# The first norm of a two-block layer stack: order of the identity, the norm weights' copy and the first square

## What is computed

```
def _rms_norm(x, g):
    xf = x.astype(jnp.float32)
    y = xf * lax.rsqrt(jnp.mean(xf * xf, axis=-1, keepdims=True) + EPS)
    return (y * g.astype(jnp.float32)).astype(x.dtype)

h = _rms_norm(x, g_pre_mix[l])
proj = h @ w_in[l]
qa, ka, va, c_q, c_kv, k_r, gate_logits = _split_cols(proj, ...)
...
x = x + _rms_norm(merged @ w_out[l], g_post_mix[l])
h2 = _rms_norm(x, g_pre_mlp[l])
m = jnp.square(jax.nn.relu(h2 @ w_up[l])) @ w_down[l]
x = x + _rms_norm(m, g_post_mlp[l])
...
return second_block(x, ...)
```

## Time and profile before

| | |
|---|---|
| Runs, median of 3 | 997.12 us (996.72 to 998.54) |
| The profiled execution | 995.95 us |
| its span in the profile | 994.2 us |
| PE busy | 978.6 us, 98% |
| DVE busy | 701.8 us, 71% |
| ACT busy | 480.0 us, 48% |
| POOL busy | 79.2 us, 8% |
| mean granted TensorE clock | 0.998 of full speed |

### The profile page before, as it was taken

The page is one execution under the profiler, slowest core; times in us unless marked ns, Lnnn a source line. Parts: engine busy times, 40 slices in busy tenths (PEclk is TensorE's granted clock), DMA queues, the critical chain, the costliest instruction groups (busy, mean ns, idle before and its releaser), DMA issues.

```text
span 994.2 us, 13319 instructions
## 1 busy us (share of the span) xinstructions
PE 978.6 (98%) x5444; PEld 851.5 (86%) x5444; DVE 701.8 (71%) x733; ACT 480.0 (48%) x558; POOL 79.2 (8%) x74
## 2 busy tenths in 40 slices
PE   8999999999999999999999999999989999999997
PEld 7888888888888888999988888888889888888886
DVE  5765657777766676567677876767789977767674
ACT  4667456554533455441235443434369745434342
POOL 0400000000000001008510000000013100000000
PEclk9999999999999999999999999999999999999999
DMA  7664424655555553652224755555245637555631
GB/s 268 228 253 161 162 87 149 212 212 186 195 202 208 183 212 142 239 171 85 85 85 162 263 187 196 184 193 193 85 148 178 248 141 266 184 196 181 201 121 42
DMA packets 27292, 176.35 MB, mean 177 GB/s; under 512 B 3416, under 2 KB 3680, under 8 KB 7648
## 3 DMA queue, kind: packets, MB, share of 16 engines
q1 hardware_dynamic: 27072, 175.44, 50.1%
q10 hardware_dynamic: 160, 0.07, 0.0%
HBM read 174.45 MB, written 1.05 MB: 177 GB/s over the span
## 4 chain that ended last, share of the span: by engine, by line
PE 87%; DVE 7%; ACT 2%; issue 2%; DMA 2%; POOL 0%; ACTq 0%; POOLq 0%; DVEq 0%; SPq 0%
PE ps L1682 20%; PE ps L1655 16%; PE ps L1657 16%; PE ps L1656 16%; PE ps L1685 10%; PE ps L2065 3%; DVE wL L995 2%; PE ps L1701 2%; DMA raw<-w_stream 1%; PE ps L1839 1%; ACT FF L558 1%; DVE FF L1587 1%; PE ps L1735 1%; PE ps L1849 1%; DVE RR L1007 1%
## 5 line engine op out<-in xcount | busy, mean ns | idle before, releaser
L995 DVE TENSOR_TENSOR wL<-raw,wH 128x2048 fp32r<-128x2048 f32 (+2 forms) x158 | 352.8, 2242 | 92.2 <-ACT wH L553 92.1
L553 ACT ACTIVATE wH<-raw 128x2048 fp32r<-128x2048 f32 (+2 forms) x158 | 292.7, 1859 | 121.2 <-PE ps L1685 54.3
L1682 PE MATMUL ps<-aHL,wH 128*128 128x512 f32 x864 | 215.8, 392 | 0.0
L1682 PEld LDWEIGHTS ps<-aHL,wH 128*128 128x128 f32 x864 | 157.2, 189 | 29.4
L1655 PE MATMUL ps<-wL,RR 128*128 128x512 f32 (+1 forms) x384 | 150.2, 391 | 0.4 <-DVE RR L1007 0.4
L1656 PE MATMUL ps<-wH,RR 128*128 128x512 f32 (+1 forms) x384 | 149.2, 389 | 0.0
L1657 PE MATMUL ps<-wH,RR 128*128 128x512 f32 (+1 forms) x384 | 148.9, 388 | 0.0
L1685 PEld LDWEIGHTS ps<-aHL,wL 128*128 128x128 f32 x864 | 117.9, 190 | 8.4
L1685 PE MATMUL ps<-aHL,wL 128*128 128x256 f32 x864 | 120.5, 282 | 0.0
L1655 PE MATMUL ps<-wL,aHL 128*128 128x512 f32 (+2 forms) x296 | 119.1, 402 | 0.2 <-ACT xn L567 0.2
L1657 PE MATMUL ps<-wH,aHL 128*128 128x512 f32 (+2 forms) x296 | 114.0, 385 | 0.0
(11 more groups left out here) (237 smaller groups left out, 1138.2 us busy)
## 6 DMA issues: line engine op xcount, KB each, us to landing
raw<-w_stream SPq DMA_DIRECT2D x152, 1024.0 KB, 4.9
raw<-w_stream SPq DMA_DIRECT2D x6, 512.0 KB, 4.6
FF<-rows_in SPq DMA_DIRECT2D x5, 512.0 KB, 6.9
raw<-w_stream SPq DMA_DIRECT2D x4, 576.0 KB, 5.4
bc<-rows_in SPq DMA_DIRECT2D x4, 512.0 KB, 7.5
xr<-x_in SPq DMA_DIRECT2D x2, 512.0 KB, 4.0
xn<-rows_in SPq DMA_DIRECT2D x1, 1024.0 KB, 4.8
out<-xn SPq DMA_DIRECT2D x4, 256.0 KB, 2.2
```

The costliest lines, as they stand in the source:

```text
L553: e.activation(weight_slot(i)[0][:, 0:wd], raw[:, slot, 0:wd], ACT.Copy).then_inc(hi, 1)
L995: e.tensor_tensor(l[:, 0:wd], raw[:, slot, 0:wd], h[:, 0:wd].bitcast(F32), ALU.subtract).then_inc(lo, 1)
L1682: e.matmul(ps[:, b, :], h[:, cs[k]], aHL[:, k].rearrange("p i t -> p (i t)"), start=k == 0, stop=False)
```

## The change

Three places are written in another order, and the number of products of zeros goes from 11 to 12. ACT issues the identity first and the norm weights second. ACT takes the first square (tile 0) ahead of the copy of the turned norm weights, while the squares of tile 1 stay behind it. PE makes eight products of zeros, waits for x's first tile, makes two more, then the gain product, then two more; before, it made six, the gain product, two, waited for x's first tile, and made three. All waits and all other instructions of the kernel are kept.

```
--- before.py
+++ after.py
@@ -567,8 +567,8 @@
                 e.activation(dst, ps[:, bank, 0:width], ACT.Copy).then_inc(copied, 1)
 
 
+            e.dma_start(ident[:, :], const_d[:, 0:128]).then_inc(id_in, 16)
             e.dma_start(gain_rows, rows_d[R_PRE_MIX:R_PRE_MIX + 1024].rearrange("(k p) -> k p", k=8)).then_inc(gain_in, 16)
-            e.dma_start(ident[:, :], const_d[:, 0:128]).then_inc(id_in, 16)
             e.wait_ge(dve_own, 2)
             e.activation(consts[:, 2:3], consts[:, 1:2], ACT.Square).then_inc(act_own, 1)
 
@@ -584,10 +584,10 @@
                 e.wait_ge(gained, GAINED["mix", t, g])
                 e.activation(aH[:, 4 * g:4 * g + 4, TOK[t]], plain_rows[:, t, 4 * g:4 * g + 4], ACT.Copy).then_inc(flip_hi, 1)
 
+            e.wait_ge(x_in[0], 16)
+            square(("mix", 0, 0), first_out[:, 0], xr[:, 0, 0:512])
             e.wait_ge(gain_out, 1)
             e.activation(gain_cols, ps[:, 7, 0:8], ACT.Copy).then_inc(gain_act, 1)
-            e.wait_ge(x_in[0], 16)
-            square(("mix", 0, 0), first_out[:, 0], xr[:, 0, 0:512])
             e.wait_ge(x_in[1], 16)
             for c in range(2):
                 square(("mix", 1, c), first_out[:, 2 + c], xr[:, 1, 512 * c:512 * c + 512])
@@ -1716,13 +1716,13 @@
                     e.matmul(ps[:, 0, 0:128], warm, warm, start=True, stop=True)
 
             e.wait_ge(warm_in, 1)
-            warm_up(6)
+            warm_up(8)
+            e.wait_ge(x_in[0], 16)
+            warm_up(2)
             e.wait_ge(gain_in, 16)
             e.wait_ge(id_in, 16)
             e.matmul(ps[:, 7, 0:8], gain_rows, ident[0:8, 0:8], start=True, stop=True).then_inc(gain_out, 1)
             warm_up(2)
-            e.wait_ge(x_in[0], 16)
-            warm_up(3)
 
 
             ck = a_at("w_in", 1536, 384, 8)
```

## The result

The changed kernel took 993.27 us (median of 5 runs, 992.86 to 994.21) against 997.12 for the kernel before (5 runs, 996.23 to 998.80) on the same chip: a ratio of 0.9959, with a 95% interval of 0.9945 to 0.9974. Measured again beside other kernels it was 993.48 (9 runs) against 996.39 (28 runs), ratio 0.9973 (0.9963 to 0.9983). So it is 2.9 to 3.9 us faster. The lower end is the better figure: of the kernel before there are 70 runs beside the experiments, with a median of 996.50, and the five here, with 997.12, lie above it. The forecast was 994.9 and 2.2 us, with a range of 993.5 to 996.5: the direction was right, the saving too small, and the time is 0.2 us outside the range.

What follows compares the result with a forecast made beforehand. PE was taken as the bound, its front strung on the identity's transfer. Shift 2.1 us plus 0.1 for the clock made 2.2; 995.95 less 2.2, plus 1.17 to the median, gave 994.9 us, range 993.5 to 996.5.

Steps and rivals of the forecast that it cites:

- What bounds: Whole kernel: PE busy 98% of the span; at the front it waits 2.1 us for the identity's landing.
- Part 1: ACT's first square ahead of the copy: x lands at 4.4, transposes possible at 6.67 instead of 8.88.
- Part 2: ACT's transfers, identity ahead of norm weights: weights land about 5.2 to 5.3, at the latest 5.83.
- late-weights rival: Norm weights land at 5.83 as the identity did; saves 1.4 to 1.7 us, 995.5; chance 0.20.
- Part 3: PE's products of zeros: wait for x costs nothing, gain product at about 5.45, PE ready for transposes at 6.95.
- Part 4: Tile 1's statistics on DVE: mean done at 7.78, L1103 at 7.8 to 8.07 against 10.00; 2.1 us taken.
- What follows: After L1735: weights land early enough and the stream shifts along, so 2.1 us is carried to the end.
- absorbed: Rival: a wait further on takes the shift back, 997.1; chance 0.06.
- slower: Rival: weights stuck behind the first burst, landing at 10.8, L1103 3.5 us late, 1000.6; chance 0.04.
- slow clock: Rival: clock stays low into L1735 in the changed kernel, 1.7 of 2.2 us lost, 996.6; chance 0.10.
- The clock: PE's clock at the front: rise expected before 8.6; 0.1 us added for low pace, bounds 0 and 1.0.
- The sum: Profiled execution 995.95 less 2.2 is 993.75; plus 1.17 from that execution to the median, 994.9.

Runs made afterwards that it cites:

- the kernel with the pause put back: Changed kernel with six products of zeros ahead of the gain product and none between the wait for x and it: 994.05 us, ratio to before 0.9978.
- The filled kernel: Kernel before with ten products of zeros ahead of the gain product instead of six, nothing else changed: 995.03 us against 996.60, ratio 0.9986.
- the square alone: Kernel before with only ACT's first square moved ahead of the copy of the transposed weights: 995.92 us, ratio 0.9995.

## Why the prediction was wrong

The mechanism of the shift was right, and the steps up to L1735 came out within 0.4 us each. Two terms of the sum failed: the 0.1 us for the clock, and the 1.17 us from the profiled execution to the median, which was carried over unchanged.

- What bounds: as said, PE, with the identity's transfer at the front. That wait is gone.
- Part 1: the landing of x, put at 4.4 with 4.54 as its upper bound, was at 4.76, and at 4.90 in the second profile. The 4.32 that the forecast started from was itself early. By the start of DVE's square, the tile is there at 4.31 to 4.55 in six profiles with the old order of transfers (mean 4.41) and at 4.61 to 4.90 in six with the new one (mean 4.75), so the identity costs x's first tile 0.34 us in the mean, not 0.22.
- Part 2: in the changed kernel the gain product waited for no transfer. Where it asks earlier, in the kernel with the pause put back, the weights are what it waits for, and they are there at 4.90, earlier than the 5.2 to 5.3 of the forecast. The late-weights rival falls.
- Part 3: it started at 5.78, not 5.45, because the last four zeros waited for x's late landing (4.78). The wait that was called free made it 0.3 us late. The transposes at 7.02 are 0.07 from the 6.95 that was worked out, though by another way: PE was ready early and DVE's rows were late.
- Part 4: L1103 at 7.76 behind the mean of tile 1 (7.78 was forecast for it). That it fits so well is luck: the gain product was 0.33 us late, but its copy came 0.42 us behind it instead of 0.60, at the upper level of the clock, and the mean 0.74 behind the second square's start instead of 0.83.
- What follows: the shift was carried to the end, as assumed. The absorbed and slower rivals fall, and so does the slow clock: the first six of L1735 took 2.20 us in both profiles of the changed kernel. That rival's price was also too high by its own row. The 1.7 us read off are what the clock withheld over 4 us; the kernel lost about 0.6.
- The clock: this is the term of the sum that was mis-sized. It stood in it with 0.1 us and bounds of 0 and 1.0. By the profiles the pace of L1735's first six costs the kernel before 0.43 us in the mean (0, 0.26 and 1.02), and the changed kernel nothing; by the runs, putting the pause back into the changed kernel costs 0.65 us of span, and filling it in the kernel before gains 1.2. The slow clock was looked for on the wrong side: as a rival for the changed kernel, when it was the kernel before that paid it. That its one profile showed L1735 at full pace was taken for the rule.
- The sum: "The median of the runs is 1.17 above that execution, so 994.9" failed as well. The 1.17 came from three runs with a median of 997.12. The 70 later ones have a mean 0.77 above that execution: 0.42 in the span, though it had the low stretch at 740 us in it, and 0.35 outside it (1.75 us against 2.10). The changed kernel has next to none of either: its medians are 0 and 0.27 above its two profiled executions. Counted from execution to execution, the sum's 993.75 is 0.5 above the measured 993.27, which is the low stretch at 740 us. Counted from mean to mean, 996.72 less 2.24 (L1735), 0.43 (its pace) and 0.30 (outside the span) is 993.75, and 993.65 was measured.
- Chance of the low stretch at 740 us: it is in the profile of before and not in that of the changed kernel, and makes their difference 0.5 us larger than the shift (2.7 against 2.2). Two of three profiles of before don't have it either, so it comes and goes with the execution there. Whether the change makes it rarer is not shown: two profiles of the changed kernel without it are too few.

The Trainium skill ("TensorE: Matmul & The Clock Gate", Part 1: What's actually happening) says that the lower clock is the resting state and activity lifts it. The times agree: filling the pause gained 1.6 us in the median, moving it to just ahead of the transposes lost 1.0. The filled kernel's one profile doesn't show an earlier rise, though. The rule of its Part 4 on transposes was weighed in the forecast as speaking for a slow clock; the changed kernel has only two products between gain product and transposes, and its transposes ran at the upper level (1.10 us for eight).

What stays open: the 0.3 us outside the span. That time is 2.10 in the mean for the kernel before, 2.20, 1.98 and 1.89 for the three kernels with its products of zeros (six, the gain product, two, the wait for x, three), and 1.79 to 1.83 for all with others. In the kernel before it is up to 3.41 us in single runs, in the changed kernel never over 1.85. All three profiled executions of before have 1.75 or 1.76, so no trace of it shows the excess, and no experiment took the order apart. Also open is why the fill gives 1.2 us of span when the pace of L1735's first six explains only 0.43. An earlier rise of the clock in other executions of the filled kernel, with quick zeros and an earlier L1735 as in the profile of the square alone, would do it, but no profile of the filled kernel shows one.

## What to carry to other kernels

One profile is one draw of the clock's state. Where TensorE pauses for a microsecond or two in the first ten, look at the granted clock and at the pace of the first matmuls in several executions, and price the pause as the difference between them, not by the one at hand. Don't carry the distance between a profiled execution and the median over to a changed kernel when the change touches what makes the scatter. Products of zeros paid in the first pause, ahead of the first real work: four of them there gained 1.6 us. Where the last of them were moved ahead, so that 1.22 us of idle stood in front of the transposes, the kernel lost 1.0 us, and ten instructions of them behind the gain product held the transposes for 2.50 us at the lower level. In the pause at 735 us five gained nothing that can be told.

## What the runs showed of the hardware

- The clock can rise early, and fall again while the work runs: granted 0.51 and 0.53 of full speed over 7.5 to 11 us in two kernels with a pause of 1.00 and of 2.11 us ahead of the gain product. In both, the gain product and the zeros behind that pause had run at the upper level (0.35 us for the product, where the lower level takes 0.56).
- A stretch at 1.2 GHz behind a pause of 1.9 us at 735 us was there in six of twelve executions and cost about 0.6 us net. None of 44 runs without a pause of 1 us ahead of the first real work had a mean granted clock under 0.997; with such a pause, 13 of 70, 3 of 10 and 8 of 11 did in three kernels, and 1 of 33 in three others.
- A transfer of 64 KB issued by ACT within 10 ns of SP's first (0.71 and 0.72) put off the landing of that 512 KB one by 0.34 us in the mean of six profiles against six (4.61 to 4.90 against 4.31 to 4.55), more than its own packets' 0.22 us. Issued by SP right behind it, it did not (4.27 and 4.20).
- The small transfer of 8 rows, issued second at 1.16 to 1.18, had landed when the gain product started at 4.90 to 5.13 us in three kernels, so it waits less than the 64 KB one did in the same place (5.83).
